# A hybrid decoder step on one core: sample keys, output copies and state updates in another order

## The reference

```python
p = x @ lp['w_in']                      # 2048 x 6412: RWKV-7, retention and mLSTM heads together
...                                     # token mixing of the three head groups, each with its state
mix = jnp.concatenate([o_rw, o_ret, o_ml], -1).astype(x.dtype) @ lp['w_out']
x1 = _layernorm(ALPHA * x + mix, lp['ln1_g'], lp['ln1_b'])
hdn = jax.nn.silu(x1 @ lp['w_gate']) * (x1 @ lp['w_up'])
x2 = _layernorm(ALPHA * x1 + hdn @ lp['w_down'], lp['ln2_g'], lp['ln2_b'])
```

```python
scores = jnp.einsum('bcihd,bcjhd->bchij', qc, kc) * dmask
y = jnp.einsum('bchij,bcjhv->bcihv', scores, vc)
kv = jnp.einsum('bcjhd,bcjhv->bchdv', k_end, vc)
def step(rs, kv_c):
    return chunk_decay * rs + kv_c, rs
y = y + jnp.einsum('bcihd,bchdv->bcihv', q_dec, r_before)
```

## Time and profile before

| | us |
|---|---|
| median of 3 runs | 2979.08 (2970.36 to 2984.87) |
| the profiled execution | 2977.48 |
| its span, first to last instruction | 2975.7 |
| TensorE busy in the span | 2846.6 (96%) |
| TensorE weight loads busy | 2732.7 (92%) |
| VectorE busy | 1615.9 (54%) |
| ScalarE busy | 1179.8 (40%) |
| mean granted TensorE clock | 0.963 of full speed |

### The profile page before, as it was taken

One profiled execution on the slowest core, in us unless ns is written; L12 is line 12 of the kernel. 1 busy time (PEld: TensorE's weight loads), 2 busy tenths in 40 slices (PEclk: granted clock), 3 DMA queues, 4 the chain that ended last, 5 costly groups with the idle time before them and its releaser, 6 DMA issues.

```text
span 2975.7 us, 56241 instructions
## 1 busy us (share of the span) xinstructions
PE 2846.6 (96%) x23683; PEld 2732.7 (92%) x23683; DVE 1615.9 (54%) x1674; ACT 1179.8 (40%) x1455; POOL 0.2 (0%) x4
## 2 busy tenths in 40 slices
PE   6999998999999999999999999988999999999995
PEld 5988897979999999999998989877999999999995
DVE  5546536459645545454584575364785454554444
ACT  4335323426433333333363453233463333333333
POOL 0000000000000000000000000000000000000000
PEclk9999998999999999999999999988899999999997
DMA  5624322526555555554564532242555555555551
GB/s 164 190 82 143 94 79 66 163 90 184 188 179 177 176 177 177 176 181 168 183 195 123 157 110 81 70 130 79 159 178 177 179 179 177 176 177 181 174 180 62
DMA packets 278664, 445.02 MB, mean 150 GB/s; under 512 B 45124, under 2 KB 75646, under 8 KB 278182
## 3 DMA queue, kind: packets, MB, share of 16 engines
q1 hardware_dynamic: 276888, 439.29, 47.4%
q10 hardware_dynamic: 1600, 3.12, 0.3%
HBM read 430.58 MB, written 11.78 MB: 149 GB/s over the span
## 4 chain that ended last, share of the span: by engine, by line
PE 89%; DVE 6%; ACT 3%; issue 2%; DMA 0%; ACTq 0%; DVEq 0%
PE psum L639 19%; PE psum L640 19%; PE psum L638 19%; PE psum L671 7%; PE psum L672 6%; PE psum L673 6%; DVE w_lo L1578 1%; ACT w_hi L1203 1%; PE psum L868 1%; PE psum L661 1%; PE psum L662 1%; PE psum L663 1%; PE psum L1015 1%; PE psum L1030 1%; PE psum L826 1%
## 5 line engine op out<-in xcount | busy, mean ns | idle before, releaser
L1574 DVE TENSOR_TENSOR w_lo<-w_raw,w_hi 128x1024 fp32r<-128x1024 f32 x496 | 605.6, 1225 | 704.8 <-ACT w_hi L1190 703.7
L1190 ACT ACTIVATE w_hi<-w_raw 128x1024 fp32r<-128x1024 f32 x508 | 538.4, 1060 | 930.1 <-PE psum L640 920.9
L638 PE MATMUL psum<-x_hi,w_lo 128*128 128x264 f32 (+3 forms) x3072 | 879.0, 286 | 6.6 <-DVE x_lo L1776 6.6
L640 PE MATMUL psum<-x_hi,w_hi 128*128 128x264 f32 (+3 forms) x3072 | 879.7, 286 | 0.0
L639 PE MATMUL psum<-x_lo,w_hi 128*128 128x264 f32 (+3 forms) x3072 | 878.9, 286 | 0.0
L638 PEld LDWEIGHTS psum<-x_hi,w_lo 128*128 128x128 f32 x3072 | 582.2, 190 | 8.0 <-issue 7.3
L639 PEld LDWEIGHTS psum<-x_lo,w_hi 128*128 128x128 f32 x3072 | 581.5, 189 | 0.2
L640 PEld LDWEIGHTS psum<-x_hi,w_hi 128*128 128x128 f32 x3072 | 580.5, 189 | 0.0
L1578 DVE TENSOR_TENSOR w_lo<-w_raw,w_hi 128x1024 fp32r<-128x1024 f32 x304 | 368.8, 1222 | 271.3 <-ACT w_hi L1203 251.2
L671 PE MATMUL psum<-x_hi,w_lo 128*128 128x264 f32 (+1 forms) x1376 | 420.1, 305 | 27.6 <-ACT p_ml L1230 14.8
L1203 ACT ACTIVATE w_hi<-w_raw 128x1024 fp32r<-128x1024 f32 x292 | 304.3, 1055 | 329.1 <-PE psum L673 263.4
(11 more groups left out here) (439 smaller groups left out, 2673.5 us busy)
## 6 DMA issues: line engine op xcount, KB each, us to landing
w_raw<-in_w_in SPq DMA_DIRECT2D x192, 512.0 KB, 3.6
w_raw<-in_w_gate SPq DMA_DIRECT2D x176, 512.0 KB, 3.5
w_raw<-in_w_up SPq DMA_DIRECT2D x176, 512.0 KB, 3.6
w_raw<-in_w_down SPq DMA_DIRECT2D x176, 512.0 KB, 4.1
w_raw<-in_w_out SPq DMA_DIRECT2D x64, 512.0 KB, 4.0
w_raw<-in_w_in SPq DMA_DIRECT2D x16, 262.0 KB, 2.8
r_sample<-in_state_ret SPq DMA_DIRECT2D x6, 512.0 KB, 7.7
out_s_ret<-r_sample SPq DMA_DIRECT2D x6, 512.0 KB, 6.3
```

The source lines that it names most:

```text
L638: mm(out, w1, bh[:, k, 0:nt], start=(k == 0), stop=False)
L640: last = mm(out, w0, bh[:, k, 0:nt], start=False, stop=(k == last_k))
L1190: A(wh[:, j, :, :], raw[:, j, :, :], ACT.Copy).then_inc(S.hi_ready, 1)
L1574: TT(wl[:, j, :, :], raw[:, j, :, :], wh[:, j, :, :].bitcast(F32), ALU.subtract).then_inc(S.lo_ready, 1)
```

## The change

What it does:

- `a_kv_sample` gets a place of its own (it lay over the scores), and VectorE builds it right behind the multiplication of the scores, before the first numerators.
- In the first chunk `a_y` is copied directly behind the carried state, and the slab that stood between them comes after.
- In the second chunk `a_y` is copied first. The three updates of the carried state stand behind the value streams.
- In mLSTM the first pair of sample states is scaled before the value streams, the other two behind the carried state.
- The table has 5 tiles before `vt` in place of 14 and 10 before `v0` in place of 8 (retention), 6 in place of 13 and 14 in place of 16 (mLSTM). Everything behind `v0` comes 7 and 9 tiles earlier, and the tiles that are left run behind `spread1`.
- Two waits are new on TensorE: `vt` waits until both chunks' numerators are copied, and in retention pair 1 waits until the state is kept, since bank 7 is read until then.

```diff
@@ -260,7 +260,7 @@
     rrot = at("r_rotary", O_H, [128, 2, T])
     pml = at("p_ml", P_RET, [128, 16, T])
 
-    kvs = at("a_kv_sample", B0 + 15552, [128, AP_ + 1, AH * NS])
+    kvs = at("a_kv_sample", P_I + 16384, [128, AP_ + 1, AH * NS])
     kst = at("a_k_turned", B0 + 15552 + 1024, [AH * NS, AP_, 128])
     vst = at("a_v_streams", B0 + 6336, [AH * NS, NS, 128])
     msam = at("m_sample", Z, [128, AP_, NS, 128])
@@ -424,7 +424,7 @@
                [(f'w{c}', 3), (f'u{c}', 3), (f'out{c}', 3)]
 
     ret_steps = [('shift', 30), ('swap', 6), ('swap1', 5), ('turn0', 91), ('turn1', 5), ('score', 5), ('num0', 4), ('num1', 5),
-                 ('vt', 14), ('v0', 8), ('v1', 4), ('v2', 4), ('sy', 4), ('sumsq', 6), ('spread', 9), ('spread1', 5)]
+                 ('vt', 5), ('v0', 10), ('v1', 4), ('v2', 4), ('sy', 4), ('sumsq', 6), ('spread', 9), ('spread1', 5)]
     rw_last = [('sa', 25), ('sv', 7), ('sy', 19), ('gn', 5), ('gnss', 8), ('gnsp', 9)]
     rw_steps = [
         [('in', 0), ('a', 7), ('g', 7), ('kk', 11), ('kks', 9), ('bonus', 15)] +
@@ -432,7 +432,7 @@
         [('in', 0), ('a', 7), ('g', 7), ('kk', 11), ('kks', 9), ('v', 80), ('bonus', 6)] +
         chunk_steps(0, 24) + chunk_steps(1, 10) + rw_last]
     ml_steps = [('spread_m', 14), ('spread_e', 12), ('turn0', 14), ('turn1', 5), ('score', 5), ('num0', 9), ('num1', 11),
-                ('vt', 13), ('v0', 16), ('v1', 5), ('v2', 5), ('sy', 7), ('sumsq', 13), ('spread', 16), ('spread1', 6)]
+                ('vt', 6), ('v0', 14), ('v1', 5), ('v2', 5), ('sy', 7), ('sumsq', 13), ('spread', 16), ('spread1', 6)]
     OUT_A = 20
     RET_POS, RW_POS, OUT_POS = OPEN, OPEN + RET_FILL, IN_GROUPS
 
@@ -845,6 +845,7 @@
 
                 bg.to('vt')
                 pe.wait_ge(S.a_kv_sample, n + 1)
+                pe.wait_ge(S.a_y_kept, 2 * n + 2)
                 for i in range(AP_ + 1):
                     last = tr(ps[0:AH * NS, 4 + i // AP_, 128 * (i % AP_):128 * (i % AP_) + 128], kvs[:, i, :], ident)
                 last.then_inc(S.a_kv_turned, 1)
@@ -854,6 +855,8 @@
                         pe.wait_ge(S.a_kv_ready, 2 * n + 2)
                     elif ml or p > 1:
                         pe.wait_ge(S.a_pair_done, n * AP_ + (p if ml else 1))
+                    else:
+                        pe.wait_ge(S.a_state_kept, 2 * n + 2)
                     for b in range(2):
                         last = mm(ps[:, (4 if ml or p != 1 else 6) + b, :], kst[:, p, :],
                                   vst[:, 4 * b:4 * b + 4, :].rearrange("p b v -> p (b v)"), start=True, stop=True)
@@ -1800,21 +1803,6 @@
                         dve.wait_ge(S.m_exp, l + 1)
                     w = ssb[:, c, :, :] if ml else rdec[:, 0:AH, :]
                     TT(pairs(ssb[:, c, :, :]), halves_of(4 + 2 * c, CH, AH), pairs(w), ALU.mult).then_inc(S.a_weighted, 1)
-                for c in range(NCH):
-                    bg.to(f'num{c}')
-                    dve.wait_ge(S.a_summed, 2 * n + c + 1)
-                    if c == 0:
-                        then(v.tensor_copy(st[:, 0, :, :], ps[:, 7, 0:384].rearrange("p (a b) -> p a b", a=AP_)))
-                    else:
-                        for p in range(AP_):
-                            sc = mdc[:, p:p + 1] if ml else gam[:, AP_ + p:AP_ + p + 1]
-                            then(STT(st[:, 1, p, :], st[:, 0, p, :], sc, ps[:, 7, 128 * p:128 * p + 128], ALU.mult, ALU.add))
-                    dve.sem_inc(S.a_state_kept, 1)
-                    y = v.tensor_copy(pairs(ay[:, :, CH * c:CH * c + CH]), halves_of(4, CH, AH))
-                    y.then_inc(S.a_y_kept, 1)
-                dve.wait_ge(S.a_y_kept, 2 * n + 2)
-
-                dve.wait_ge(S.a_sample_loaded, 48 * (n + 1))
                 sam = msam if ml else rsam
                 k = kw[:, :, SEQ:T] if ml else src[:, AP_:2 * AP_, SEQ:T]
                 by_head = sums[:, AH * AH:AH * AH + AP_ * AH].rearrange("p (a h) -> p a h", h=AH)
@@ -1823,13 +1811,31 @@
                        k.unsqueeze(2).to_broadcast([128, AP_, AH, NS]), ALU.mult))
                 v.tensor_copy(kvs[:, AP_, :].rearrange("p (h b) -> p h b", b=NS),
                               src[:, 2 * AP_:2 * AP_ + AH, SEQ:T]).then_inc(S.a_kv_sample, 1)
+                for c in range(NCH):
+                    bg.to(f'num{c}')
+                    dve.wait_ge(S.a_summed, 2 * n + c + 1)
+                    if c == 0:
+                        own(v.tensor_copy(st[:, 0, :, :], ps[:, 7, 0:384].rearrange("p (a b) -> p a b", a=AP_)))
+                        dve.sem_inc(S.a_state_kept, 1)
+                    y = v.tensor_copy(pairs(ay[:, :, CH * c:CH * c + CH]), halves_of(4, CH, AH))
+                    y.then_inc(S.a_y_kept, 1)
+                    if c == 0:
+                        bg.step()
+                dve.wait_ge(S.a_sample_loaded, 48 * (n + 1))
                 if ml:
-                    for p in range(AP_):
-                        then(TT(sam[:, p, :, :], sam[:, p, :, :], over(msk[:, p, :], 128), ALU.mult))
+                    own(TT(sam[:, 0, :, :], sam[:, 0, :, :], over(msk[:, 0, :], 128), ALU.mult))
                 bg.to('vt')
                 dve.wait_ge(S.a_kv_turned, n + 1)
                 TT(vst[:, :, :], each(ps[0:AH * NS, 5, 0:128], NS), over(same, 128),
                    ALU.mult).then_inc(S.a_kv_ready, 1)
+                dve.wait_ge(S.a_y_kept, 2 * n + 2)
+                for p in range(AP_):
+                    sc = mdc[:, p:p + 1] if ml else gam[:, AP_ + p:AP_ + p + 1]
+                    then(STT(st[:, 1, p, :], st[:, 0, p, :], sc, ps[:, 7, 128 * p:128 * p + 128], ALU.mult, ALU.add))
+                dve.sem_inc(S.a_state_kept, 1)
+                if ml:
+                    for p in range(1, AP_):
+                        own(TT(sam[:, p, :, :], sam[:, p, :, :], over(msk[:, p, :], 128), ALU.mult))
                 for p in range(AP_):
                     bg.to(f'v{p}')
                     dve.wait_ge(S.a_vspread, n * AP_ + p + 1)
```

## The result

The changed kernel takes 2957.3 us (median of 7 runs, 2952.1 to 2961.5), the kernel before 2979.1 (2970.4 to 2990.0). The ratio is 0.9921, with an interval of 0.9903 to 0.9939: 0.8% faster, and with 21.8 us about four times the 5.6 us that I had forecast. Two more sets of runs of the same program gave 0.9946 [0.9930, 0.9961] and 0.9914 [0.9893, 0.9936]. The profiled execution took 2959.8 us.

The account below looks back on a forecast made before the run. TensorE, busy 2846.6 of 2975.7 us, was taken as the bound. Terms -4.2 - 6.2 - 3.0 - 0.7 + 7.6 + 0.7 + 0.5 = -5.3 us gave 2972.2 profiled and 2973.5 us as median, range 2963 to 2983.

Parts of the forecast that it names:

- What goes away: TensorE's four waits vanish: first numerators -4.2 us, sample keys -6.2, pairs of sample states -3.0, a `p_ret` group -0.7.
- Tile 120: mLSTM, behind the sums of squares: a new TensorE wait of 3.8 us in each layer, +7.6 us, ends 2.6 and 4.3.
- Tile 80: mLSTM: TensorE waits for ScalarE's copies of group two, +0.7 us for two, between 0 and 1.8.
- Retention, pair 1: Outer products in retention: TensorE must wait until the state is kept; taken as 0, with 0 to 1.5 us per layer.
- The end of the mLSTM part: Last wait, for the fourth group's copies: +0.5 us added in layer two, 0 to 2.
- The clock: TensorE's clock after pauses: two waits of 3.1 us removed and two of 3.8 added were set equal, so no change.
- no larger gain can come from these waits: The four TensorE waits whose releaser the change moves total 14.1 us, 0.5% of the time, taken as the gain's limit.
- the first one: Rival: both new long waits drop the clock once, 2 x 1.7 = 3.4 us, giving 2977 us; chance 0.18.
- the rule that I had weighed with it: Trainium skill: the gate lets half the pulses through unless TensorE was busy of late; sum 3.4 us less favourable.
- both clock rivals: New long waits slow TensorE's clock: one stretch each (2977 us, chance 0.18), or three per layer (2984 us, chance 0.10).
- The second one: Rival: the wait at tile 120 keeps the clock low, 5.1 us lost per layer, 2984 us, slower; chance 0.10.
- The third one: Rival: the wait at tile 120 does not come since ScalarE copies in time, 2964.6 us; chance 0.15.

## Why the prediction was wrong

The forecast was 2973.5 us with a range down to 2963; it came to 2957.3. Step by step:

- **What goes away**: right. The earlier trace rows are gone to the last wait, -14.1 us, and the 1.1 us at L1143 with them.
- **Tile 120**: right, 3.83 us for 3.8. **Tile 80**: 0.4 us for 0.35. **Retention, pair 1**: right, no wait; what I feared there, from 0 to 1.5 us, is just what the old table brings with the new order, 1.2 us.
- **The end of the mLSTM part**: +0.5 taken, 0 to 2 allowed; the row for L661 says +2.9 in the profiled execution (+1.0 and +2.8 in those of the other two sets), against 1.1 saved at L1143.
- The sum at full clock: -5.3 predicted, -4.7 ± 0.6 measured. (The way from there to the forecast, 2972.2 + 1.6, gives 2973.8 and not 2973.5, which changes nothing.)
- **The clock** is the step that failed: "I remove two waits of 3.1 us and add two of 3.8 us; in the sum I set these equal". That puts the clock at zero. Measured are 17.1 ± 1.3 us. I priced pauses by their length, from the three cases of the earlier trace rows, and looked at the long ones alone. What the runs show in its place is the clock behind the short waits: the four of 0.85 and 1.25 us ahead of the numerators, to which I gave 4.2 us, carry 8.5 ± 2.3 us of clock on top when they alone are taken from the kernel before, and 16.8 ± 1.9 when they alone are put back into the changed one, 2 to 4 us each in the mean. The row was in the trace before: 10 us at 0.51 from 1610.6, two microseconds behind such a wait. I did not look at the clock behind the small waits of the earlier trace rows. Why the same waits cost twice as much among the new edits stays open.
- The bound "no larger gain can come from these waits" (14.1 us) was wrong for the same reason: a wait's row in the table does not hold the clock that it costs.
- The rivals: the first one's price for the new waits was right where they stand, 1.7 us each forecast and 1.7 to 2.6 read, and the rule that I had weighed with it says the same. As a forecast for the kernel both clock rivals have the wrong sign, since they look at the new long waits only. The second one's 5.1 us for each layer behind the sums is reached in one of the six parts that the three profiles of the changed kernel show (10.2 us at half clock); the others have 1.7 to 3.4. The third one's time (2964.6) came nearest, but by a mechanism that did not occur.

## What to carry to other kernels

Price a pause of the busy engine together with the clock behind it (here stretches of 3.4 to 27 us), and do not leave out the short ones, above all those right beside sparse work (narrow or small multiplications). Here about 1 us of waiting cost 2 to 6 us of clock in the mean, and 3.8 us among dense tiles about 2; such a stretch does not follow every time. A copy that another engine waits for goes ahead of background work, even where the wait is under a microsecond. To test such a cause, fill the pause with useless work no longer than the pause: if the loss to the clock falls, the pause's clock was the price.

## What was not expected

- 1.2 us of waiting ahead of the second outer product was followed by 27 us at half clock in three of the four places that the two profiles with this wait show; without it about the same work ran at 0.75.
- Where the slow stretches lie in code that is the same changes from one execution to the next: at 43 us, ahead of anything that the change touches, there were 6.8 us of it in the kernel before and none in the changed one. One profile's clock therefore says little.
- One of the fill's multiplications, 128 columns with float32 factors, takes 0.22 us (7.6 us for 34). It is two instructions in the profile (x68 for 34), of 0.11 us each; I had taken the time of one instruction for that of a multiplication.
- The sums of squares moved by 8 tiles take away 10 us at full clock and give back 5.0 ± 2.5 to the clock. Which stretch takes them is open.
